# A hybrid mLSTM and attention layer on one core: the order of attention pairs, of output gates and of numerator matmuls is changed

## The chip, the core and the metric

The kernel runs on one NeuronCore of a Trainium2 chip, as one program. The time is the device time of one execution in microseconds (us), the median over runs. The engines are PE (TensorE, matmuls), ACT (ScalarE), DVE (VectorE) and the DMA queues that SP issues. Each works through its own list of instructions in order and waits on semaphores for the others.

## The reference

One trunk layer for 128 prompt tokens and 512 latent tokens, 640 in all, with the same weights:

- a half-step SwiGLU feed-forward, then two token mixers side by side, then a second half-step feed-forward;
- mixer A is a bidirectional mLSTM: for each chunk and direction the output is `num / max(|den|, exp(-m))`, where `num = (q k^T * decay) v + w * (q C)`: a part that comes from the values of the chunk, and a part that comes from the state `C` carried in;
- mixer B is grouped attention, 16 query heads on 4 key heads of 64 dimensions, rotary positions on latent tokens. Prompt tokens read the 128 prompt keys, latent tokens read 512 latent and 128 cached keys;
- `y = g0 * (hm @ w_bm) + g1 * (ha @ w_ba)`, with `hm` the mLSTM output times the sigmoid of its output gate, and then `y @ w_out`.

All weights and inputs are float32.

## The kernel before

The 640 tokens lie along the free axis, the 1024 channels in 8 blocks of 128 partitions. A projection by one block of 128 output channels is a *weight tile*: SP loads it (`raw`), ACT copies a rounded high part (`whi`, line L839), DVE subtracts for a low part (`wlo`, L1167), and PE multiplies in three terms (L458, L459, L460), twice 320 columns for each of 8 blocks. Each engine's program is a fixed list written out in order in Python; no scheduler moves anything. The attention order comes from one counter k, which every engine turns into tokens and heads for itself.

The three places that the change touches:

**The mLSTM units.** 20 units, n = 0 to 19, one for each tile of 128 tokens (5) and pair of heads (4). The first four belong to the prompt tile, which starts from no state. In each unit PE does half a weight tile, spreads m (L645, L654), multiplies keys by queries (L658), does the second half of the weight tile, and then runs `nums_of(n)`: for two heads (`hh`) and two directions (`d`) a value matmul (L670, all 128 rows of the array) and, unless c = 0, a state matmul into the same place of PSUM (L673, 64 rows: rows 0 to 63 for hh = 0, 64 to 127 for hh = 1). Every one is float32 and shows as two instructions in the trace. `turn_hm(n-1)` (L681) follows. DVE prepares `sa` and `qw` (`decays`, L1482 to L1492), and divides (`outputs`, L1501 to L1515; `scale_hm`, L1520).

**The query projections.** Ten weight tiles for keys and queries; after each one PE sums squares (L706) and swaps halves (L707), ACT forms an inverse root (`inv_rms`, L1049, L1051), and DVE rotates (`turn_halves`, L1540 to L1546).

**The attention pairs.** 40 pairs (`PAIRS`), k = 0 to 39: tile c = k // 8 (0 is the prompt), head pair m = k % 8. For each, PE computes scores (`scores`: L746 for the prompt, L751 and L754 for latent tokens, K = 64 in two halves of the array), turns the normalised weights (`turn_p`, L768: one block of 128 for each head of a prompt pair, five for a latent one) and multiplies by the values (`values`, L778). DVE takes the maximum (`top`, L1566), copies turned blocks (`take_second`, L1580, L1583), divides (`divide`, L1571, L1573) and splits the output (`low_ha`, L1590). ACT copies the other turned block (`take_p`, L1081), takes exponentials (L1094), and copies the high part (`high_ha`, L1086). On PE the order is scores(k+1), turn_p(k), [fill], values(k). A `fill` is a quarter of a weight tile of the m branch (12 matmuls, L798 to L800); there are 32, and they go beside pairs 8 to 39. The fills read h_hi and h_lo, which are made from `hm` beside the first pairs: DVE gates it (`out_gate`, L1596, pairs 0 to 7), ACT copies the high part (L1099), DVE subtracts (`low_m`, L1602, pairs 1 to 8). ACT splits a weight tile after each fourth pair (`k % 4 == 3`), DVE one pair later; `take_fill` (L1612) empties the fill's bank.

Of the kernel before, what the change touches and what calls it, by code (L numbers as in the profile page):

```python
# [17 lines left out]
ALU = mybir.AluOpType  # L18
# [3 lines left out]
P = 128  # L22
D = 1024
KC = D // P
TP, TS = 128, 512
N = TP + TS
# [36 lines left out]
UNITS = NT * 4  # L63
PAIRS = NT * KC

# [23 lines left out]
def build(nc, a):  # L89
    ctx = ExitStack()  # L90
    with ctx:
# [351 lines left out]
        def _(pe):  # L443
# [217 lines left out]
            def nums_of(n):  # L661
                c, j = n // 4, n % 4
                pe.wait_ge(s_in, n + 1)
                if n >= 1:
                    pe.wait_ge(den_s, 4 * n)
                for hh in range(2):
                    half = slice(hh * DK, (hh + 1) * DK)
                    for d in range(2):
                        out = psum[:, hh, d * (DV + 1):(d + 1) * (DV + 1)]
                        last = mm(out, sa[n % 2][:, (2 * d + hh) * P:(2 * d + hh + 1) * P], vt[:, c, 2 * j + hh, :],  # L670
                                  start=True, stop=(c == 0))
                        if c > 0:
                            last = mm(out, qw[half, n % 2, d, :], cs[half, d, c - 1, j, :], start=False, stop=True)  # L673
                last.then_inc(nums, 1)
# [34 lines left out]
            for l in range(L_AV, L_BM):  # L709
# [18 lines left out]
                if l > L_AK:  # L728
                    qk_stats(l - 1 - L_AK)
            qk_stats(QK - 1)  # L730


            def scores(k):
                c, m = k // KC, k % KC
                if k >= 1:
                    pe.wait_ge(aexp, 2 * k)
                else:
                    pe.wait_ge(ck_ev, 2)
                    pe.wait_ge(ak_sw, 32)
                    pe.wait_ge(rope_out, QK)  # L740
                half = [slice(s * HD, (s + 1) * HD) for s in range(2)]
# [19 lines left out]
            def turn_p(k):  # L761
                c = k // KC
                if k >= 1:
                    pe.wait_ge(ha_lo, k)
                for s in range(2):
                    pe.wait_ge(p_nrm, 2 * k + s + 1)
                    for b in range(1 if c == 0 else NT):
                        last = tp(turned(s, b), sa[s][:, b * P:(b + 1) * P], ident)  # L768
                    last.then_inc(atr, 1)

            def values(k):
                c, m = k // KC, k % KC
                pe.wait_ge(pta, k + 1)
# [9 lines left out]
            def fill(f):  # L783
# [17 lines left out]
                if part == 1:  # L801
                    last.then_inc(tile_done if h else half_done, 1)

            scores(0)
            for k in range(PAIRS):
                if k + 1 < PAIRS:
                    scores(k + 1)
                turn_p(k)
                if k >= KC:
                    fill(k - KC)  # L810
                values(k)
# [21 lines left out]
        def _(act):  # L833
# [219 lines left out]
            for l in range(L_AV, L_BM):  # L1053
# [17 lines left out]
                if l > L_AK:  # L1071
                    inv_rms(l - 1 - L_AK)
            inv_rms(QK - 1)

            def take_p(k):
                c = k // KC
                w = P if c == 0 else TS
# [5 lines left out]
            def high_ha(k):  # L1083
                c, m = k // KC, k % KC
                act.wait_ge(pv, k + 1)
                fn(m_hi[:, m, c * P:(c + 1) * P], psum[:, T_LAST, 2 * P:3 * P], ACT.Copy, scale=0.5).then_inc(ha_hi, 1)  # L1086

            def exponentials(k, s):
                c = k // KC
                w = P if c == 0 else N  # L1090
# [13 lines left out]

            act.preload_act_table_set("exp_and_others")
            exponentials(0, 0)
            exponentials(0, 1)
            for k in range(PAIRS):
                take_p(k)
# [46 lines left out]
        def _(dve):  # L1156
# [377 lines left out]
            scale_hm(UNITS - 1)  # L1534

            def turn_halves(e):
                dst = qk(e)
# [10 lines left out]
            for l in range(L_AV, L_BM):  # L1548
# [9 lines left out]
                if l > L_AK:  # L1558
                    turn_halves(l - 1 - L_AK)
            turn_halves(QK - 1)  # L1560


            def top(k, s):
                w = P if k < KC else N
                dve.wait_ge(sc, k + 1)
                dve.tensor_reduce(amax[:, s:s + 1], flat(s)[:, 0:w], AX.X, ALU.max, negate=True).then_inc(nmx, 1)  # L1566

            def divide(k, s):
                w = P if k < KC else N
                dve.wait_ge(aexp, 2 * k + s + 1)  # L1570
# [4 lines left out]
            def take_second(k):  # L1575
                w = P if k < KC else TS
                dve.wait_ge(atr, 2 * k + 2)
                if k >= 1:
                    dve.wait_ge(pv, k)
                last = copy(sb[1][:, 0:w], psum[:, T_BANK + 1, 0:w])  # L1580
                if k >= KC:
                    for s in range(2):
# [3 lines left out]
            def low_ha(k):  # L1586
                c, m = k // KC, k % KC
                dve.wait_ge(ha_hi, k + 1)
                cols = slice(c * P, (c + 1) * P)
                stt(m_lo[:, m, cols], psum[:, T_LAST, 2 * P:3 * P], 0.5, m_hi[:, m, cols].bitcast(F32),  # L1590
                    ALU.mult, ALU.subtract).then_inc(ha_lo, 1)

            def out_gate(m):
                dve.wait_ge(gate_in[m], 16)
                dve.wait_ge(hm_ev, UNITS)
                stt(hm[:, m, :], hm[:, m, :], 0.5, gate[m][:, :], ALU.mult, ALU.mult).then_inc(mg, 1)  # L1596
                dve.wait_ge(mg, m + 1)
                dve.sem_inc(gate_used, 1)

# [18 lines left out]
            for k in range(PAIRS):  # L1618
                top(k, 0)
                top(k, 1)  # L1620
                if k >= 1:
                    take_second(k - 1)
                divide(k, 0)
                divide(k, 1)
                if k >= 1:
                    low_ha(k - 1)
                if k < KC:
                    out_gate(k)
                if 1 <= k <= KC:
# [139 lines left out]
```

## Time and profile before

| | |
|---|---|
| time, median of 3 runs | 1977.47 us (1976.69 to 1982.18) |
| time of the profiled execution | 1979.02 us |
| its span | 1977.2 us |
| granted TensorE clock, mean | 0.972 |
| PE busy | 1873.5 us, 95% |
| DVE busy | 941.7 us, 48% |
| ACT busy | 651.2 us, 33% |
| chain that ended last | PE 86%, DVE 7%, ACT 4%, issue 2% |

PE carries the chain. Its clock has two levels; PEclk 1.00 is 2.4 GHz and 0.50 is 1.2 GHz. The mLSTM units lie from about 770 to 1011 us, the key and query projections to 1117 us, the attention pairs from 1124 to 1340 us.

### The profile page before, as it was taken

Reading aid. Unit: us, or ns where it says so; the run is one execution under the profiler, and the core shown is the slowest. Engines: PE = TensorE matmul, PEld = TensorE weight load, DVE = VectorE, ACT = ScalarE, POOL = GpSimd, SP = SyncE. Lnnn points to the kernel's source line nnn. Section 1 sums busy time; section 2 is a strip of 40 time slices with the busy share of each in tenths; the row PEclk is TensorE's granted clock in tenths of the full one; section 3 lists DMA queues with packets and bytes.
Section 4 is the critical chain, followed back from the end, with each engine's and each line's share of the span. In section 5 each row is a group of like instructions: output and inputs, shape, how many; then the busy total and the mean of one; then the engine's idle time right before and its main releaser. Section 6 shows DMA issues by size and latency. Waiting matters only on the chain.

```text
span 1977.2 us, 31472 instructions
## 1 busy us (share of the span) xinstructions
PE 1873.5 (95%) x12888; PEld 1778.8 (90%) x12888; DVE 941.7 (48%) x1578; ACT 651.2 (33%) x1067; POOL 0.2 (0%) x4
## 2 busy tenths in 40 slices
PE   6999999999968999999999789999979999999996
PEld 6999999999958998888889668889969999999996
DVE  4765465542674234444434587784354222222235
ACT  3422222112453123433323455452453222221233
POOL 0000000000000000000000000000000000000000
PEclk9999999999979999999989889999989999999997
DMA  7444444422321224222232211112312222222211
GB/s 299 148 153 129 135 157 133 133 75 95 128 85 58 72 72 98 71 69 70 70 118 83 62 52 36 36 36 71 129 43 65 74 75 75 74 75 75 72 56 54
DMA packets 52294, 178.38 MB, mean 90 GB/s; under 512 B 8521, under 2 KB 11099, under 8 KB 51427
## 3 DMA queue, kind: packets, MB, share of 16 engines
q1 hardware_dynamic: 52195, 176.97, 28.0%
q8 instruction: 72, 1.18, 0.3%
q14 instruction: 27, 0.22, 0.0%
HBM read 162.40 MB, written 13.90 MB: 89 GB/s over the span
## 4 chain that ended last, share of the span: by engine, by line
PE 86%; DVE 7%; ACT 4%; issue 2%; DMA 0%; SPq 0%; DVEq 0%; ACTq 0%
PE psum L458 22%; PE psum L460 22%; PE psum L459 22%; PE psum L778 2%; PE psum L768 2%; PE psum L500 2%; PE psum L673 1%; PE psum L751 1%; PE psum L670 1%; PE psum L489 1%; ACT whi L839 1%; DVE x L1202 1%; PE psum L645 1%; DVE macc L1231 1%; DVE amax L1566 1%
## 5 line engine op out<-in xcount | busy, mean ns | idle before, releaser
L458 PE MATMUL psum<-h_hi,whi 128*128 128x320 f32 x2288 | 718.3, 314 | 9.0 <-DVE wlo L1167 7.5
L459 PE MATMUL psum<-h_lo,whi 128*128 128x320 f32 x2288 | 708.4, 310 | 0.0
L460 PE MATMUL psum<-h_hi,wlo 128*128 128x320 f32 x2288 | 708.4, 310 | 0.0
L1167 DVE TENSOR_TENSOR wlo<-raw,whi 128x1024 fp32r<-128x1024 f32 x213 | 260.7, 1225 | 804.3 <-ACT whi L839 804.2
L458 PEld LDWEIGHTS psum<-h_hi,whi 128*128 128x128 f32 x2288 | 431.2, 188 | 15.6 <-DVE wlo L1167 7.8
L459 PEld LDWEIGHTS psum<-h_lo,whi 128*128 128x128 f32 x2288 | 431.3, 188 | 1.9 <-issue 1.9
L460 PEld LDWEIGHTS psum<-h_hi,wlo 128*128 128x128 f32 x2288 | 430.9, 188 | 0.0
L839 ACT CAST whi<-raw 128x1024 fp32r<-128x1024 f32 x213 | 222.3, 1044 | 380.4 <-PE psum L460 370.2
L458 PE MATMUL psum<-g_hi,whi 128*128 128x320 f32 x704 | 218.2, 310 | 1.2 <-DVE g_lo L1296 1.2
L459 PE MATMUL psum<-g_lo,whi 128*128 128x320 f32 x704 | 217.6, 309 | 0.0
L460 PE MATMUL psum<-g_hi,wlo 128*128 128x320 f32 x704 | 217.5, 309 | 0.0
L1231 DVE SCALAR_TENSOR_TENSOR macc<-mw,silc,macc 128x512 f32<-128x512 f32 x210 | 142.7, 744 | 0.0
L458 PEld LDWEIGHTS psum<-g_hi,whi 128*128 128x128 f32 x704 | 132.3, 188 | 1.7 <-DVE g_lo L1296 1.7
L459 PEld LDWEIGHTS psum<-g_lo,whi 128*128 128x128 f32 x704 | 132.2, 188 | 0.0
L460 PEld LDWEIGHTS psum<-g_hi,wlo 128*128 128x128 f32 x704 | 132.2, 188 | 0.0
L917 ACT ACTIVATE sa<-psum 128x640 f32<-128x640 f32 x44 | 31.0, 705 | 151.4 <-PE psum L460 148.4
L778 PE MATMUL psum<-sb,av 128*64 128x128 f32 x672 | 47.3, 284 | 18.3 <-DVE sb L1580 12.4
L923 ACT CAST g_hi<-sb 128x640 f32 x44 | 32.1, 729 | 93.2 <-DVE sb L1290 93.2
L778 PEld LDWEIGHTS psum<-sb,av 128*64 128x64 f32 x672 | 37.0, 139 | 27.6 <-issue 26.5
L1094 ACT ACTIVATE sa<-psum,amax 128x640 f32<-128x640 f32 (+1 forms) x80 | 56.1, 709 | 13.1 <-DVE amax L1566 13.1
L1566 DVE TENSOR_REDUCE amax<-psum 128x1 f32<-128x640 f32 (+1 forms) x80 | 53.5, 711 | 14.0 <-PE psum L754 12.7
L1296 DVE TENSOR_TENSOR g_lo<-sb,g_hi 128x640 f32 x44 | 36.2, 823 | 36.8 <-ACT g_hi L923 36.8
(218 smaller groups left out, 2027.0 us busy)
## 6 DMA issues: line engine op xcount, KB each, us to landing
raw<-in_w_ffn_in SPq DMA_DIRECT2D x88, 512.0 KB, 3.5
raw<-in_w_mix SPq DMA_DIRECT2D x77, 512.0 KB, 3.7
mw<-in_w_mod SPq DMA_DIRECT2D x28, 768.0 KB, 4.7
raw<-in_w_ffn_out SPq DMA_DIRECT2D x32, 512.0 KB, 3.5
mw<-in_w_mod SPq DMA_DIRECT2D x4, 2048.0 KB, 19.5
gate<-gate_keep SPq DMA_DIRECT2D x24, 320.0 KB, 4.1
mw<-in_w_mod SPq DMA_DIRECT2D x14, 512.0 KB, 3.7
gate_keep<-gate SPq DMA_DIRECT2D x20, 320.0 KB, 4.6
```

Of the source, the lines that this page charges most:

```text
L458: mm(out, whi[t.slot][:, k, :], hi[:, k, cols], start=(k == 0), stop=False)
L459: mm(out, whi[t.slot][:, k, :], lo[:, k, cols], start=False, stop=False)
L460: last = mm(out, wlo[t.slot][:, k, :], hi[:, k, cols], start=False, stop=(k == nk - 1))
L500: last = mm(mod_out(2 * t + g, bank), macc[:, g, t * P:(t + 1) * P], ones_d, start=True, stop=True)
L768: last = tp(turned(s, b), sa[s][:, b * P:(b + 1) * P], ident)
L778: last = mm(psum[s * HD:(s + 1) * HD, T_LAST, 2 * P:3 * P], av[:, v, (m // 2) * HD:(m // 2 + 1) * HD], sb[s][:, b * P:(b + 1) * P], start= ...
L839: copy(whi[t.slot][:, :, :], raw[t.raw][:, :, :]).then_inc(w_hi, 1)
L1094: fn(sa[s][:, 0:w], flat(s)[:, 0:w], ACT.Exp, bias=amax[:, s:s + 1], accum_out=asum[:, s:s + 1]).then_inc(aexp, 1)
L1167: tt(wlo[t.slot][:, :, :], raw[t.raw][:, :, :], whi[t.slot][:, :, :].bitcast(F32), ALU.subtract).then_inc(raw_free, 1)
L1231: last = stt(acc, w[:, k, :], by, acc, ALU.mult, ALU.add)
L1296: tt(g_lo[:, jj, :].rearrange("p o n -> p (o n)"), sb[s][:, :], g_hi[:, jj, :].rearrange("p o n -> p (o n)").bitcast(F32), ALU.subtract).t ...
L1566: dve.tensor_reduce(amax[:, s:s + 1], flat(s)[:, 0:w], AX.X, ALU.max, negate=True).then_inc(nmx, 1)
```

## The change

Three edits, in all engines' lists alike:

1. A table `ORDER` gives tile and heads for each pair. Pairs 0 to 7 are now those of the first latent tile. After them come 8 groups of four: three latent pairs and one prompt pair. The fills stay at pairs 8 to 39, ACT's weight splits at `k % 4 == 3`, which is now the prompt pair of each group. The scores of the first pair stand ahead of the last square sum and rotation.
2. `out_gate(m)` is done beside the eight query projections and no longer beside pairs 0 to 7.
3. In `nums_of`, both heads' value matmuls come first, then both heads' state matmuls of direction 0, those of direction 1, and then the value matmuls of direction 1.

```diff
+ORDER = [(1, m) for m in range(KC)]
+for i in range(KC):
+    ORDER += [(2 + n // KC, n % KC) for n in range(3 * i, 3 * i + 3)] + [(0, i)]
+PAIRS = len(ORDER)
...
@@ PE, nums_of
-                for hh in range(2):
-                    half = slice(hh * DK, (hh + 1) * DK)
-                    for d in range(2):
-                        out = psum[:, hh, d * (DV + 1):(d + 1) * (DV + 1)]
-                        last = mm(out, sa[...], vt[:, c, 2 * j + hh, :], start=True, stop=(c == 0))
-                        if c > 0:
-                            last = mm(out, qw[half, n % 2, d, :], cs[half, d, c - 1, j, :], start=False, stop=True)
+                for d in range(2):
+                    for part in ((0, 1) if d == 0 else (1, 0)):
+                        for hh in range(2):
...
@@ PE, scores
-                    pe.wait_ge(rope_out, QK)
+                if k < KC:
+                    pe.wait_ge(rope_out, NKC + m + 1)
@@ PE, turn_p
+                else:
+                    pe.wait_ge(rope_out, QK)
@@ PE
-            qk_stats(QK - 1)
+            for l in (L_BM - 2, L_BM - 1):
+                t = Tile(T_MIX + l)
+                pe.wait_ge(ev[t.slot], t.pair + 1)
             scores(0)
+            qk_stats(QK - 1)
@@ ACT
-            inv_rms(QK - 1)
-            act.preload_act_table_set("exp_and_others")
             exponentials(0, 0)
             exponentials(0, 1)
+            inv_rms(QK - 1)
+            act.preload_act_table_set("exp_and_others")
@@ DVE, beside the projections
-            turn_halves(QK - 1)
+                if l >= L_AQ:
+                    out_gate(l - L_AQ)
@@ DVE, the pairs
                 if k >= 1:
                     take_second(k - 1)
+                else:
+                    turn_halves(QK - 1)
...
-                if k < KC:
-                    out_gate(k)
```

What stands on PE in one mLSTM unit, before (n = 4; L670 are value matmuls, L673 state matmuls, L681 the turn of the unit before):

```order
L670 MATMUL psum<-vt,sa_70 128x129
L673 MATMUL psum<-cs,qw 128x129
L670 MATMUL psum<-vt,sa_70 128x129
L673 MATMUL psum<-cs,qw 128x129
L670 MATMUL psum<-vt,sa_70 128x129
L673 MATMUL psum<-cs,qw 128x129
L670 MATMUL psum<-vt,sa_70 128x129
L673 MATMUL psum<-cs,qw 128x129
L681 MATMUL psum<-cst,hmt 128x128 x2
L458 MATMUL psum<-h_hi,whi_67 128x320
```

and after, at the same place (the lines are now L675, L678, L686, L461):

```order
L463 MATMUL psum<-h_hi,wlo_68 128x320
L675 MATMUL psum<-vt,sa_70 128x129 x2
L678 MATMUL psum<-cs,qw 128x129 x4
L675 MATMUL psum<-vt,sa_70 128x129 x2
L686 MATMUL psum<-cst,hmt 128x128 x2
L461 MATMUL psum<-h_hi,whi_67 128x320
```

The eight matmuls are the same; between 128 rows and 64 rows the list changed eight times (the change to L681 counted), and now it changes twice.

What stands on DVE where the projections end and the pairs begin, before (L1540 to L1546 rotate the last queries, L1566 is the maximum of pair 0, L1596 the gate):

```order
L1540 TENSOR_TENSOR sb_72<-psum,cst 128x512
L1541 TENSOR_TENSOR aq<-aq,cst 128x512
L1543 TENSOR_TENSOR aq<-aq,sb_72 128x512
L1546 TENSOR_TENSOR aq<-aq,rb 128x640
L1566 TENSOR_REDUCE amax<-psum 128x1 x2
L1571 RECIPROCAL arec<-asum 128x1
L1573 TENSOR_SCALAR sa_70<-sa_70,arec 128x128
L1571 RECIPROCAL arec<-asum 128x1
L1573 TENSOR_SCALAR sa_71<-sa_71,arec 128x128
L1596 SCALAR_TENSOR_TENSOR hm<-hm,gate_119 128x640
L1566 TENSOR_REDUCE amax<-psum 128x1 x2
```

and after (L1550 is the last gate, L1585 the maximum, L1558 to L1564 the last rotation, L1590 and L1592 the division of pair 0):

```order
L1550 SCALAR_TENSOR_TENSOR hm<-hm,gate_126 128x640
L1585 TENSOR_REDUCE amax<-psum 128x1 x2
L1558 TENSOR_TENSOR sb_72<-psum,cst 128x512
L1559 TENSOR_TENSOR aq<-aq,cst 128x512
L1561 TENSOR_TENSOR aq<-aq,sb_72 128x512
L1564 TENSOR_TENSOR aq<-aq,rb 128x640
L1590 RECIPROCAL arec<-asum 128x1
L1592 TENSOR_SCALAR sa_70<-sa_70,arec 128x640
L1590 RECIPROCAL arec<-asum 128x1
L1592 TENSOR_SCALAR sa_71<-sa_71,arec 128x640
L1585 TENSOR_REDUCE amax<-psum 128x1 x2
```

The eighth gate and the first maximum now stand ahead of the last rotation, and the first pair is a latent one (640 columns instead of 128).

## Rows read from the trace of the kernel before

**Rows 1.** Busy time by stage: stretch, length, PE, PEld, DVE, ACT, POOL, PEclk, DMA share, GB/s.

```profile
885.00:1005.00 120.00, 118.83 (x713) 101.97 (x712) 52.53 (x142) 37.43 (x101) 0.00 (x0) 1.00 0.23 66
1127.00:1152.00 25.00, 13.98 (x72) 7.35 (x68) 21.49 (x68) 12.84 (x47) 0.00 (x0) 0.50 0.33 92
1158.00:1330.00 172.00, 166.14 (x1624) 148.59 (x1622) 136.80 (x324) 84.95 (x195) 0.00 (x0) 1.00 0.11 36
```

**Rows 2.** Timeline, PE, unit 9, numerators: start, duration, instruction, [idle before].

```profile
886.20 0.38 PE L670 MATMUL psum<-vt,sa 128*128 128x129 f32 x2
886.51 0.49 PE L673 MATMUL psum<-cs,qw 64*128 64x129 f32 x2
...
889.43 0.44 PE L681 MATMUL psum<-cst,hmt 128*128 128x128 f32 x2
```

**Rows 3.** Timeline, PE, a unit of the prompt tile, value matmuls alone.

```profile
801.49 1.05 PE L670 MATMUL psum<-vt,sa 128*128 128x129 f32 x8
802.38 0.38 PE L681 MATMUL psum<-cst,hmt 128*128 128x128 f32 x2
```

**Rows 4.** Timeline, PE, two K = 64 matmuls side by side, then the projection.

```profile
882.16 0.49 PE L658 MATMUL psum<-mq,mk 64*128 64x128 f32 x4
882.58 0.41 PE L458 MATMUL psum<-h_hi,whi 128*128 128x320 f32 x1
```

**Rows 5.** Timeline, DVE and PE around the numerators of that unit.

```profile
883.66 0.75 DVE L1492 TENSOR_TENSOR sa<-sa,psum 128x256 f32<-128x256 f32 x2 [0.37 <-ACT sa L1007]
888.06 1.23 DVE L1167 TENSOR_TENSOR wlo<-raw,whi 128x1024 fp32r<-128x1024 f32 x1 [3.65 <-ACT whi L839]
892.68 0.42 DVE L1520 TENSOR_TENSOR hmt<-hmt,ss 128x256 f32<-128x256 f32 x1 [1.33 <-ACT ss L1018]
893.31 1.12 PE L645 MATMUL psum<-nm,rowc 8*128 8x256 f32 x4
```

**Rows 6.** Timeline of the last unit on PE, and the clock of the stretch it starts in.

```profile
1004.82 0.77 PE L670 MATMUL psum<-vt,sa 128*128 128x129 f32 x2 [1.17 <-DVE sb L1510]
...
1010.61 0.69 PE L681 MATMUL psum<-cst,hmt 128*128 128x128 f32 x2
```

```profile
1004.00:1008.00 4.00, 3.18 (x9) 2.30 (x10) 1.52 (x4) 1.71 (x8) 0.00 (x0) 0.58 0.75 213
```

**Rows 7.** Timeline, PE and DVE, the first scores and the second pair's maximum.

```profile
1124.43 0.80 PE L746 MATMUL psum<-ak,aq 64*128 64x128 f32 x4 [3.06 <-DVE aq L1546]
...
1127.85 0.49 DVE L1566 TENSOR_REDUCE amax<-psum 128x1 f32<-128x128 f32 x2 [0.15 <-DVE hm L1596]
```

**Rows 8.** Timeline, a latent pair with a fill (k = 10 and its neighbours), PE and DVE.

```profile
1161.38 1.31 PE L778 MATMUL psum<-sb,av 128*64 128x128 f32 x20
1162.62 1.14 PE L751 MATMUL psum<-ak,aq 64*128 64x256 f32 x8
1163.90 1.31 PE L768 MATMUL psum<-cst,sa 128*128 128x128 f32 x10
1164.02 1.55 DVE L1566 TENSOR_REDUCE amax<-psum 128x1 f32<-128x640 f32 x2 [0.69 <-PE psum L754]
1166.09 0.48 DVE L1583 COPY sb<-psum 128x128 f32<-128x128 f32 x2
1166.91 1.31 PE L778 MATMUL psum<-sb,av 128*64 128x128 f32 x20
```

**Rows 9.** Timeline, DVE, maximum of the last pair, k = 39.

```profile
1330.63 1.55 DVE L1566 TENSOR_REDUCE amax<-psum 128x1 f32<-128x640 f32 x2 [0.29 <-PE psum L754]
```

**Rows 10.** Timeline, ACT and DVE, the cast and subtraction of hm beside a prompt pair.

```profile
1148.48 0.72 ACT L1099 CAST h_hi<-hm 128x640 fp32r<-128x640 f32 x1
...
1149.78 0.83 DVE L1602 TENSOR_TENSOR h_lo<-hm,h_hi 128x640 fp32r<-128x640 f32 x1
```

**Rows 11.** The scores of the first latent pair, and the clock behind them.

```profile
1151.97 2.08 PE L751 MATMUL psum<-ak,aq 64*128 64x256 f32 x8
```

```profile
1154.00:1156.00 2.00, 1.02 (x8) 0.48 (x4) 1.86 (x3) 0.88 (x2) 0.00 (x0) 0.80 0.63 161
```

More of the change, by code:

```diff
@@ L63 @@
 UNITS = NT * 4
-PAIRS = NT * KC
+ORDER = [(1, m) for m in range(KC)]
+for i in range(KC):
+    ORDER += [(2 + n // KC, n % KC) for n in range(3 * i, 3 * i + 3)] + [(0, i)]
+PAIRS = len(ORDER)
 STATES = ((0, 0), (1, 0), (0, 1), (1, 4), (0, 2), (1, 3), (0, 3), (1, 2))
@@ L665, in nums_of @@
                     pe.wait_ge(den_s, 4 * n)
-                for hh in range(2):
-                    half = slice(hh * DK, (hh + 1) * DK)
-                    for d in range(2):
-                        out = psum[:, hh, d * (DV + 1):(d + 1) * (DV + 1)]
-                        last = mm(out, sa[n % 2][:, (2 * d + hh) * P:(2 * d + hh + 1) * P], vt[:, c, 2 * j + hh, :],
-                                  start=True, stop=(c == 0))
-                        if c > 0:
-                            last = mm(out, qw[half, n % 2, d, :], cs[half, d, c - 1, j, :], start=False, stop=True)
+                for d in range(2):
+                    for part in ((0, 1) if d == 0 else (1, 0)):
+                        for hh in range(2):
+                            half = slice(hh * DK, (hh + 1) * DK)
+                            out = psum[:, hh, d * (DV + 1):(d + 1) * (DV + 1)]
+                            if part == 0:
+                                last = mm(out, sa[n % 2][:, (2 * d + hh) * P:(2 * d + hh + 1) * P], vt[:, c, 2 * j + hh, :],
+                                          start=(d == 0 or c == 0), stop=(d == 1 or c == 0))
+                            elif c > 0:
+                                mm(out, qw[half, n % 2, d, :], cs[half, d, c - 1, j, :], start=(d == 1), stop=(d == 0))
                 last.then_inc(nums, 1)
@@ L729, in _ @@
                     qk_stats(l - 1 - L_AK)
-            qk_stats(QK - 1)
             def scores(k):
-                c, m = k // KC, k % KC
+                c, m = ORDER[k]
                 if k >= 1:
@@ L761, in turn_p @@
             def turn_p(k):
-                c = k // KC
+                c = ORDER[k][0]
                 if k >= 1:
                     pe.wait_ge(ha_lo, k)
+                else:
+                    pe.wait_ge(rope_out, QK)
                 for s in range(2):
@@ L771, in values @@
             def values(k):
-                c, m = k // KC, k % KC
+                c, m = ORDER[k]
                 pe.wait_ge(pta, k + 1)
@@ L1072, in _ @@
                     inv_rms(l - 1 - L_AK)
-            inv_rms(QK - 1)
             def take_p(k):
-                c = k // KC
+                c = ORDER[k][0]
                 w = P if c == 0 else TS
@@ L1083, in high_ha @@
             def high_ha(k):
-                c, m = k // KC, k % KC
+                c, m = ORDER[k]
                 act.wait_ge(pv, k + 1)
@@ L1088, in exponentials @@
             def exponentials(k, s):
-                c = k // KC
+                c = ORDER[k][0]
                 w = P if c == 0 else N
@@ L1534, in _, with out_gate @@
             scale_hm(UNITS - 1)
+            def out_gate(m):
+                dve.wait_ge(gate_in[m], 16)
+                dve.wait_ge(hm_ev, UNITS)
+                stt(hm[:, m, :], hm[:, m, :], 0.5, gate[m][:, :], ALU.mult, ALU.mult).then_inc(mg, 1)
+                dve.wait_ge(mg, m + 1)
+                dve.sem_inc(gate_used, 1)
             def turn_halves(e):
@@ L1559, in _ @@
                     turn_halves(l - 1 - L_AK)
-            turn_halves(QK - 1)
+                if l >= L_AQ:
+                    out_gate(l - L_AQ)
             def top(k, s):
-                w = P if k < KC else N
+                w = P if ORDER[k][0] == 0 else N
                 dve.wait_ge(sc, k + 1)
@@ L1568, in divide @@
             def divide(k, s):
-                w = P if k < KC else N
+                w = P if ORDER[k][0] == 0 else N
                 dve.wait_ge(aexp, 2 * k + s + 1)
@@ L1575, in take_second @@
             def take_second(k):
-                w = P if k < KC else TS
+                w = P if ORDER[k][0] == 0 else TS
                 dve.wait_ge(atr, 2 * k + 2)
@@ L1580, in take_second @@
                 last = copy(sb[1][:, 0:w], psum[:, T_BANK + 1, 0:w])
-                if k >= KC:
+                if ORDER[k][0]:
                     for s in range(2):
@@ L1586, in low_ha @@
             def low_ha(k):
-                c, m = k // KC, k % KC
+                c, m = ORDER[k]
                 dve.wait_ge(ha_hi, k + 1)
@@ L1591, in low_ha @@
                     ALU.mult, ALU.subtract).then_inc(ha_lo, 1)
[L1593 to L1598, printed above, removed]
             def low_m(m):
```

## The prediction

> **What bounds the kernel.** I read the busy time by stage first, then the timeline of each stage that the change touches. In the mLSTM stage PE is busy 118.83 of 120 us at a clock of 1.00, and DVE and ACT have room: what PE saves there the kernel saves, as long as nothing else becomes late [rows 1]. In the attention stage with fills PE is busy 166.14 of 172 us. Beside the prompt pairs it is busy 13.98 of 25 us and the clock stands at 0.50: there DVE (21.49 us) sets the pace, and PE has idle time that fills cannot use, since they wait for `hm` to be split [rows 1]. So the numerators are a matter of PE time, and the new order a matter of where idle PE time lies and which clock it brings.
>
> **Numerators.** From the first value matmul at 886.20 to the turn at 889.43 the eight matmuls (16 instructions) of a unit take 3.23 us, 0.20 each [rows 2]. In a unit of the prompt tile eight such instructions in a row take 802.38 - 801.49 = 0.89 us, 0.11 each [rows 3]. The shape is the same, so half of the 3.23 us goes with the changes between 128 and 64 rows: 3.23 - 16 x 0.11 = 1.5 us over 8 changes, 0.19 each. The two K = 64 matmuls of the key-query product (4 instructions, one per half of the array, as the new state matmuls alternate) take 882.58 - 882.16 = 0.42 us with the change behind them, so 0.22 for four instructions: they run side by side, else it would be 0.44 + 0.19 [rows 4]. After the change a unit has four value matmuls, 8 x 0.11 = 0.88; four state matmuls in two pairs, 0.43; two changes, 0.38: 1.7 us. It saves 1.55, with rounding and the slower turn behind the last change (which goes too) 1.6 us.
>
> The Trainium skill (TensorEngine Tiling (Array Packing), Key Properties) says that changing the tiling mode, not just the tile, drains the engine; this agrees with 0.19 us for each change here. The same page (Gotcha 1: PSUM Pressure) says that different row tiles cannot write one PSUM bank at a time; here the two heads write banks 0 and 1, so by that rule too the pairs overlap.
>
> 16 units have state matmuls. Does DVE keep up? Its weight split stands ahead of `outputs` in its list and ends at 888.06 + 1.23 = 889.29, tied to the half tile before the numerators, not to them [rows 5]. Before, `outputs` began just after, with the end of the numerators. Now these end at 887.9, but `outputs` still begins at 889.3, 0.25 earlier than before. Its chain ends with `scale_hm` at 893.10 before and 892.85 now; the next `decays` needs that, and the spread m, which PE had ready some 1.2 us after 893.31 and now has 1.6 earlier, at 892.9. The two meet, and behind them is slack: `decays` ended at 884.41 for numerators that began at 886.20, 1.8 us later [rows 2, 5]. So 15 units save 1.6 us each, 24 us. Unit 19 is different: nothing stands between the numerators of 18 and 19 but `outputs(18)`, and that hangs on the weight split of DVE. It starts where it did, after a longer wait. Before, it waited 1.17 us and then ran from 1004.82 to 1010.61, 5.8 us, with a clock of 0.58 in that stretch [rows 6]; at the low level the new order costs twice 1.55 us, 3.1, and saves 2.7. **Sum: -27 us.** Bounds: -18 if only the drains go (6 x 0.19 x 16) and the state matmuls do not overlap; -30 if the clock stays up in unit 19 and behind it.
>
> **The gates.** Eight times 0.82 us of DVE move from the prompt pairs to the projections (the row of the same size is the subtraction, 0.83) [rows 10]. A projection takes PE about 9 us, and DVE's split, rotation and gate are some 5 us, so there it costs nothing. Only the eighth stands in the way, ahead of the first maximum.
>
> **The start.** Before, the last rotation ended at 1124.43 and the maximum of pair 1 began at 1127.85 [rows 7]. Now the rotation comes behind a gate (0.8) and two maxima of 640 columns (1.5): it ends 2.3 later, 1126.7, with some 0.2 of ACT waiting (its exponentials stand ahead of the inverse root) at 1126.9. Then two divisions of 640 columns, 1.3 us (an estimate, 2.5 times the 128-column ones is an upper bound), and the maximum of pair 1 begins at 1128.2. That is **+0.3 us**, with one latent pair half done instead of a prompt pair.
>
> **The pairs 1 to 10.** Before, from 1127.85 to the maximum of pair 10 at 1164.02: 36.2 us [rows 7, 8]. Now pairs 1 to 8 are latent (pairs 1 to 7 have no fill). What is the period of a latent pair without a fill? A closed loop goes from the first maximum to the last copy of turned blocks, 1166.57 - 1164.02 = 2.55; 0.15 to PE; values 1162.62 - 1161.38 = 1.24, and 0.12 to ACT (as from scores to maximum: 1.40 for 1.28) [rows 8]; `high_ha`, which holds ACT 0.2; the cast of hm, 0.72; the subtraction on DVE, 0.83 [rows 10]; then the next maximum. That is 5.8, and with the ends that overlap (0.1) **5.7 us**, while PE works 1.28 (scores) + 1.05 (turns, ten instructions of 0.11) + 1.24 = 3.6 of it. So the nine periods from pair 1 to pair 10 (eight like this, the last 5.3 without cast) are 51 us: **+15 us** at full clock.
>
> **The clock.** It is low at the start in both (0.50 beside the prompt pairs [rows 1], and the scores of a latent pair then take 2.08 for 1.14 [rows 8, 11]). With all PE times doubled a loop is values 2.5, scores 2.5, turns 2.1, copies and ways 1.5: 8.6 us, 2.9 more than at full clock. Before, the clock rose between 1154 and 1156, just behind the first latent pair's scores [rows 11], so here it should rise within the first two pairs: +5. But PE then idles 2.1 us in each 5.7, in one piece ahead of the values, and in the last mLSTM unit a wait of 1.17 us behind the drained numerators was followed by the low level [rows 6]. I take it to fall again once or twice, two slow pairs in all: +5. **Sum +9 us**; bounds 0 (high all along) and 8 x 2.9 = +23 (low all along).
>
> **The groups of four, pairs 10 to 39.** Before 1330.63 - 1164.02 = 166.6 us for 29 periods, 5.75 each, of which PE's work is 1166.91 - 1161.38 = 5.53 [rows 8, 9]; the rest, 0.9 us in four pairs, comes with the weight split on ACT and DVE. Now one in four is a prompt pair, one block for five: it takes off 0.95 of scores, 4/5 of 1.05 and of 1.24 of turns and values, 2.8 us. PE's work for a group is 4 x 5.53 - 2.8 = 19.3. I laid the three lists beside one another with these durations: the values behind the split still wait 0.8, since DVE takes the split ahead of the next maximum and its copies; and 0.7 more is lost where a latent pair follows a prompt pair, because PE's share of these iterations (3.7 and 4.6 us) is shorter than DVE's round of maximum, copies, divisions (5 us). 20.9 us for a group; 7.25 groups, 151.5: **-15 us**. Bounds: 19.3 (-27) and 22.1, no shorter than four latent pairs of 5.53 (-6). The last pair is a prompt pair, whose turns and values are not hidden: 0.84 + 1.0 shorter, **-2 us**.
>
> The attention stage in all: +0.3 + 15 + 9 - 15 - 2 = +7 us. With -27 it is -20: 1979.0 - 20 = 1959 in the profiled execution, whose time stands 1.5 us above the median of the runs (1977.5); so **1957.5 us**. What a measurement can tell from no change is 0.3%, 6 us.
>
> **The rivals.**
> - *The clock stays high in the new latent pairs* (0.22). For it: in the whole fill stage it is at 1.00 with PE idle 3% [rows 1]. Against: 2.1 us idle in each pair. Then +9 becomes +1 to +3: 1950.
> - *It stays low for most of the eight* (0.15). For it: with 14 of 25 us busy it stayed at 0.50 throughout [rows 1]. Against: at the low level these pairs keep PE 7.1 of 8.6 us busy, and it rose behind a single latent pair's scores. +23 for +9: 1971.
> - *The units save less, or DVE becomes their bound* (0.08): two chains meet within 0.1 us at `decays`, and 1.8 us of slack is all there is. With 1.1 for 1.6 us: 1966.
> - *The prompt pairs don't shorten their groups* (0.07): the wait moves from PE's work to DVE's round, a group stays at 22.1. -6 for -15: 1967.
> - *Slower* (0.04): the cost of a 64-row instruction is its own (it shows in both instructions of each pair, not only at the change), so the order of the numerators gives under 0.3 us a unit, -5; with the clock low for all eight pairs, the stage gives +21. 1995. It decides from 0.9 us a unit down with a low clock. Rows 3 speak against, as do rows 4.
>
> **The chances.** The forecast has 0.44 and its own range 1952 to 1965. The range of 8 in 10 takes in the high clock and most of the low one: 1946 to 1972. Faster by over 0.3% (below 1971.5) is the forecast, the high clock, both small rivals, and half of the low clock: 0.89. Within 0.3%: 0.07. Slower: 0.04.
>
> **What would show it.** In the profile after: a unit with one row of four, one of eight and one of four numerator instructions, 1.6 to 1.8 us from first to turn, and 11.0 us from unit to unit for 12.64; `outputs` right behind the weight split; the last unit's start near its old distance from unit 18's end plus 1.6. Pair periods of 5.7 (clock 1.00) or 8.6 (0.50) in the first eight, and how many of each; groups of 20.9 us with a wait ahead of the values behind each split. It is wrong if units still are over 12 us apart, if the eight pairs take over 70 us or under 45, or if groups are at 22 or at 19.5.

## The result and the profile after

The changed kernel takes 1950.63 us (median of 4 runs, 1950.55 to 1955.21), the kernel before 1978.37 beside it: ratio 0.9863, 95% interval 0.9849 to 0.9878. That is 27.7 us less; forecast were 20. The time lies inside the range of 8 in 10 (1946 to 1972) and 1.4 us below the forecast's own range (1952 to 1965), where the prediction has its rival of a high clock (1950). The profiled execution took 1955.21 us, the slowest of the four, 4.6 above their median, with a span of 1953.4 for 1977.2. Cut at marks that both traces have:

| stretch | before, us | after, us | difference | forecast |
|---|---|---|---|---|
| to the first spread of unit 0 | 769.66 | 770.66 | +1.0 | 0 |
| to the last turn, behind unit 19 | 250.2 | 223.7 | -26.5 | -27 |
| to the maximum of pair 1 | 108.0 | 108.4 | +0.4 | +0.3 |
| pair 1 to pair 10 | 36.2 | 53.3 | +17.2 | +24 (15 + 9) |
| pair 10 to pair 39 | 166.6 | 152.6 | -14.0 | -15 |
| from there to the end | 646.6 | 644.7 | -1.9 | -2 |
| span | 1977.2 | 1953.4 | -23.8 | -20 |

The first line is code that did not change; how much it varies, the first `outputs` shows: it stands at 785.3 us before, 786.3 after, and 782.1 in the first experiment, with the same instructions ahead of it. Such a difference can be the 4 us between the 23.8 of the traces and the 27.7 of the medians; the other executions of the changed kernel have no trace that would show it.

The busy time by stage, against [rows 1]: stretch, length, PE, PEld, DVE, ACT, POOL, PEclk, DMA share, GB/s. They are a piece of the mLSTM units, the latent pairs without fills, and the groups.

```profile
877.00:977.00 100.00, 100.00 (x687) 90.89 (x686) 49.15 (x136) 35.83 (x99) 0.00 (x0) 1.00 0.27 78
1103.00:1156.00 53.00, 39.05 (x389) 33.05 (x388) 42.59 (x98) 27.70 (x63) 0.00 (x0) 0.92 0.01 2
1156.00:1308.00 152.00, 142.52 (x1336) 125.38 (x1334) 115.61 (x296) 74.27 (x188) 0.00 (x0) 1.00 0.12 41
```

The middle row is the surprise: clock 0.92. Four slow pairs of 8.6 us in 60, which the forecast added up to, would give 0.71 (an estimate from its own terms).

The numerators of unit 9 in the timeline of PE (start, duration, instruction), against [rows 2]:

```profile
879.43 0.61 PE L675 MATMUL psum<-vt,sa 128*128 128x129 f32 x4
879.97 0.72 PE L678 MATMUL psum<-cs,qw 64*128 64x129 f32 x8
880.61 0.71 PE L675 MATMUL psum<-vt,sa 128*128 128x129 f32 x4
881.16 0.38 PE L686 MATMUL psum<-cst,hmt 128*128 128x128 f32 x2
```

From the first to the turn 881.16 - 879.43 = 1.73 us for 3.23. Eight value instructions take 0.88 of it and two changes 0.4, which leaves 0.45 for the eight state instructions: half of 8 x 0.11.

Is it the change of shape that costs, or that a state matmul adds into the place of PSUM that the value matmul ahead of it has just written? In the same unit before, each block of two instructions begins 0.42 us behind the last, whichever way it goes:

```profile
886.93 0.49 PE L670 MATMUL psum<-vt,sa 128*128 128x129 f32 x2
887.34 0.49 PE L673 MATMUL psum<-cs,qw 64*128 64x129 f32 x2
887.76 0.49 PE L670 MATMUL psum<-vt,sa 128*128 128x129 f32 x2
```

From L670 to L673 the place is the same, from L673 to the next L670 it is another, and both take 2 x 0.11 and 0.20. The change of shape carries the price, then, and not the shared place.

What DVE does around it, with PE's spread of m between, against [rows 5]:

```profile
881.30 1.23 DVE L1178 TENSOR_TENSOR wlo<-raw,whi 128x1024 fp32r<-128x1024 f32 x1 [3.65 <-ACT whi L850]
882.44 0.15 DVE L1512 SCALAR_TENSOR_TENSOR den<-psum,tk 128x4 f32<-128x4 f32 x1
...
884.99 1.12 PE L648 MATMUL psum<-nm,rowc 8*128 8x256 f32 x4
...
885.57 0.42 DVE L1531 TENSOR_TENSOR hmt<-hmt,ss 128x256 f32<-128x256 f32 x1 [1.33 <-ACT ss L1029]
...
886.15 1.13 DVE L1493 SCALAR_TENSOR_TENSOR sa<-psum,tk,cst 128x128 f32<-128x128 f32 x4 [0.16 <-PE psum L648]
```

`outputs` (L1512) now begins right behind the weight split, 1.3 us after its numerators ended. DVE is done with `scale_hm` (L1531) at 885.99 and waits 0.16 us for the spread: the two chains meet within 0.2 us, as forecast, and the distance from unit to unit is 11.09 us (12.64 before).

The last unit, against [rows 6], and its clock:

```profile
983.73 0.68 PE L675 MATMUL psum<-vt,sa 128*128 128x129 f32 x4 [2.39 <-DVE sb L1521]
...
986.24 0.64 PE L686 MATMUL psum<-cst,hmt 128*128 128x128 f32 x2
```

```profile
984.00:988.00 4.00, 4.00 (x23) 3.65 (x22) 1.84 (x8) 1.71 (x8) 0.00 (x0) 0.58 0.59 184
```

It waits 2.39 us for 1.17, falls to the low level in the middle, and takes 2.5 us for 5.8. Behind it the clock is at 0.98 again from 988 to 990 us; before, it stood at 0.50 from 1006 to 1014. That brings the last turn another 1.1 us nearer (8.12 us behind this one for 9.24).

The latent pairs without fills: the maxima of pairs 1, 2 and 3 on DVE, and PE's scores and values between them.

```profile
1102.77 1.54 DVE L1585 TENSOR_REDUCE amax<-psum 128x1 f32<-128x640 f32 x2
...
1105.97 2.40 PE L785 MATMUL psum<-sb,av 128*64 128x128 f32 x20 [1.27 <-DVE sb L1602]
...
1108.30 2.08 PE L756 MATMUL psum<-ak,aq 64*128 64x256 f32 x8
...
1110.86 1.56 DVE L1585 TENSOR_REDUCE amax<-psum 128x1 f32<-128x640 f32 x2 [0.70 <-PE psum L759]
...
1113.55 1.31 PE L785 MATMUL psum<-sb,av 128*64 128x128 f32 x20 [1.41 <-DVE sb L1602]
1114.79 1.13 PE L756 MATMUL psum<-ak,aq 64*128 64x256 f32 x8
...
1119.25 1.31 PE L785 MATMUL psum<-sb,av 128*64 128x128 f32 x20 [1.86 <-DVE sb L1602]
```

```profile
1116.57 0.82 DVE L1585 TENSOR_REDUCE amax<-psum 128x1 f32<-128x640 f32 x1
```

The first period, 8.09 us, runs at the low level (scores 2.08, values 2.40); the second, at the high one, takes 5.71, and so do all that follow up to pair 9 (5.70). From the third period on PE waits 1.86 us in one piece ahead of the values; the forecast had 2.1. The clock rose in this stretch:

```profile
1110.00:1112.00 2.00, 2.00 (x16) 1.59 (x14) 1.30 (x3) 0.37 (x1) 0.00 (x0) 0.76 0.00 0
```

The periods of a group are 5.15, 5.39, 5.19 and 5.33 us, 21.06 in all; the last maximum, against [rows 9], is one of 128 columns:

```profile
1308.69 0.48 DVE L1585 TENSOR_REDUCE amax<-psum 128x1 f32<-128x128 f32 x2
```

### The profile page after: what moved, and what is told of

Its sections match the earlier page's. It is cut to its first block, busy times and chain, and to the rows that moved or that the text cites. A ratio compares the mean times of both kernels' runs of the same rounds, so it can differ in the third digit from the quotient of the medians.

```text
span 1953.4 us, 31481 instructions
## 1 busy us (share of the span) xinstructions
PE 1844.7 (94%) x12888; PEld 1764.6 (90%) x12888; DVE 940.2 (48%) x1578; ACT 651.6 (33%) x1067; POOL 0.2 (0%) x4
## 4 chain that ended last, share of the span: by engine, by line
PE 83%; DVE 9%; ACT 4%; issue 3%; DMA 0%; SPq 0%; DVEq 0%; ACTq 0%
PE psum L461 23%; PE psum L462 22%; PE psum L463 22%; PE psum L785 2%; PE psum L503 2%; DVE amax L1585 1%; PE psum L775 1%; PE psum L492 1%; PE psum L756 1%; PE psum L675 1%; DVE x L1213 1%; PE psum L648 1%; DVE macc L1242 1%; DVE wlo L1178 1%; ACT whi L850 1%
## 5 line engine op out<-in xcount | busy, mean ns | idle before, releaser
L461 PE MATMUL psum<-h_hi,whi 128*128 128x320 f32 x2288 | 719.0, 314 | 9.0 <-DVE wlo L1178 7.5
L461 PEld LDWEIGHTS psum<-h_hi,whi 128*128 128x128 f32 x2288 | 431.7, 189 | 15.6 <-DVE wlo L1178 7.8
L461 PE MATMUL psum<-g_hi,whi 128*128 128x320 f32 x704 | 218.3, 310 | 1.2 <-DVE g_lo L1307 1.2
L461 PEld LDWEIGHTS psum<-g_hi,whi 128*128 128x128 f32 x704 | 132.3, 188 | 1.7 <-DVE g_lo L1307 1.7
L1585 DVE TENSOR_REDUCE amax<-psum 128x1 f32<-128x640 f32 (+1 forms) x80 | 53.5, 710 | 11.2 <-PE psum L759 11.1
L1307 DVE TENSOR_TENSOR g_lo<-sb,g_hi 128x640 f32 x44 | 36.2, 823 | 36.8 <-ACT g_hi L934 36.8
```

Of the source, the lines that this page charges most:

```text
L461: mm(out, whi[t.slot][:, k, :], hi[:, k, cols], start=(k == 0), stop=False)
L1307: tt(g_lo[:, jj, :].rearrange("p o n -> p (o n)"), sb[s][:, :], g_hi[:, jj, :].rearrange("p o n -> p (o n)").bitcast(F32), ALU.subtract).t ...
```

## The experiments

All times are medians; the ratio is to the kernel before on the same chip, with its 95% interval. The kernel before itself took 1978.4 us beside the changed kernel, 1979.1 beside e1 to e4, 1981.9 beside e5 to e8 and 1980.3 beside e9 and e10, so kernels of different groups are compared by the ratio. The last column leaves out the stretch ahead of the mLSTM units, which no edit touches and which took 766 to 771 us: it is the time in the trace from the first spread of unit 0 to the end.

| kernel | us | ratio (interval) | from unit 0 to the end, trace |
|---|---|---|---|
| kernel before | 1978.4 | 1 | 1207.6 |
| changed kernel | 1950.6 | 0.9863 (0.9849 to 0.9878) | 1182.8 |
| e1, numerators alone | 1951.1 | 0.9867 (0.9850 to 0.9883) | 1182.9 |
| e2, pairs and gates alone | 1980.8 | 1.0009 (0.9999 to 1.0018) | 1212.1 |
| e3, prompt pairs first | 1950.0 | 0.9853 (0.9837 to 0.9870) | 1178.8 |
| e4, heads apart | 1966.9 | 0.9945 (0.9928 to 0.9962) | 1195.7 |
| e5, gates back | 1955.6 | 0.9878 (0.9862 to 0.9893) | 1187.4 |
| e6, e3 and the split one pair later | 1943.0 | 0.9810 (0.9797 to 0.9824) | 1171.4 |
| e7, states by head | 1952.1 | 0.9858 (0.9840 to 0.9875) | 1182.8 |
| e8, outputs first | 1950.0 | 0.9843 (0.9826 to 0.9860) | 1180.5 |
| e9, e6 and e8 | 1939.8 | 0.9796 (0.9780 to 0.9811) | 1168.9 |
| e10, changed kernel, both moves on DVE | 1946.0 | 0.9828 (0.9813 to 0.9843) | 1177.1 |

**e1: the numerators alone.** The kernel before with `nums_of` of the changed one.

> The kernel before with the new order of the numerators alone. My theory: the order of the numerators carries nearly the whole gain. The trace after shows units 11.09 us apart for 12.64, 1.55 each, and the last unit 2.7 shorter; that is 26 us, so this kernel stands 24 to 27 us below the kernel before, near 1952. Rival: part of the gain comes from the moved gates and the new pairs; then this kernel gains under 20 us and the pairs alone over 5.

It gains 28 us, all that the changed kernel gains (24.7 us in the trace from unit 0 on, 24.8 there). Its units are 11.09 us apart; its pairs run as before (3.78 us beside the prompt, 36.2 us from pair 1 to pair 10). The rival is out.

**e2: pairs and gates alone.** The changed kernel with the old `nums_of`.

> The changed kernel with the old order of the numerators: new order of the pairs, gates beside the projections. My theory, from the two traces: start +0.3, pairs 1 to 10 +17.2, groups -14.0, end -1.9, in all +1.6 us over the kernel before, within what can be measured, -2 to +4. Rival, by the forecast's +7 for this stage (the clock falls again in the latent pairs in most executions, and the profiled one was lucky): +5 to +9. Second rival: the pairs alone gain over 5.

1.7 us slower than before, at the edge of what ten runs tell from nothing. The stage is a wash, as the table of stretches has it (+1.7). The profiled execution is the slowest of the ten, and its trace is 4.5 us above the one before from unit 0 on: 1.5 of it are a stretch at the low level inside the first units (0.60 from 776 to 780 us), and 1.4 the latent pairs. But the clock is not steady: of the nine periods from pair 1 to 10 this profile has 8.09, 6.08, 6.31 and 6.13 beside 5.70. The fall behind the wait of pair 5, in the timeline of PE and the windows:

```profile
1157.63 1.31 PE L783 MATMUL psum<-sb,av 128*64 128x128 f32 x20 [1.86 <-DVE sb L1600]
1158.87 1.91 PE L754 MATMUL psum<-ak,aq 64*128 64x256 f32 x8
```

```profile
1158.00:1160.00 2.00, 2.00 (x24) 1.67 (x22) 1.16 (x5) 0.89 (x2) 0.00 (x0) 0.77 0.00 0
1160.00:1162.00 2.00, 2.00 (x12) 1.62 (x11) 1.48 (x3) 0.00 (x0) 0.00 (x0) 0.50 0.00 0
1162.00:1164.00 2.00, 1.09 (x8) 0.85 (x6) 1.68 (x5) 1.50 (x4) 0.00 (x0) 0.88 0.00 0
```

The wait of 1.86 us ahead of it is no longer than those of the pairs before (1.87 and 1.86 at 1146.22 and 1151.92), behind which the clock stayed at 1.00, and the same as in the changed kernel. So the length of the wait does not tell when the clock falls; what does, no run here shows. The level was back about 3 us later, and a fall cost 0.4 to 0.6 us, since it covers part of a pair, and a part that had idle time. The forecast priced each at 2.9.

**e3: the prompt pairs first.**

```diff
-ORDER = [(1, m) for m in range(KC)]
-for i in range(KC):
-    ORDER += [(2 + n // KC, n % KC) for n in range(3 * i, 3 * i + 3)] + [(0, i)]
+ORDER = [(c, m) for c in range(NT) for m in range(KC)]
```

> The changed kernel with ORDER in the old sequence (prompt pairs first); the moved gates and the new numerators stay. My theory: the gates' 0.82 us on DVE were on the path beside the prompt pairs, where DVE was busy 21.5 of 25 us, so their period falls from 3.78 to about 3.0 even at the low clock; pairs 1 to 10 take 31 us for 53, pairs 10 to 39 again 166.6 for 152.6. That is 5 to 8 us less than the changed kernel, near 1944. Rival: a prompt pair's period is not DVE's work but a loop through PE at the low clock, and stays near 3.7; then this kernel is level with the changed one (-2 to +1).

Level with the changed kernel. Neither theory fits: the period of a prompt pair did fall, from 3.78 to 3.22 us (3.0 forecast), 3.1 us over the six of them from pair 1 on. But the clock, low beside the prompt pairs, rose later than before: the two periods ahead of pair 10 took 5.13 and 6.24 us for 4.15 and 5.34, which gives 1.9 back. These are windows of e3 and of e6, which runs the same instructions up to there:

```profile
1126.00:1130.00 4.00, 3.71 (x19) 2.80 (x20) 3.08 (x8) 1.80 (x6) 0.00 (x0) 0.50 0.00 0
```

```profile
1122.00:1126.00 4.00, 2.67 (x16) 1.61 (x14) 3.06 (x6) 1.85 (x5) 0.00 (x0) 0.71 0.00 0
```

In e6 the same pairs took 4.15 and 5.35, so when the clock rises differs from execution to execution by some 4 us. From pair 1 to pair 10 the two took 35.0 and 33.0 us, against 53.3 in the changed kernel; from pair 10 to 39 e3 took 166.6 against 152.6, and the end is 1.9 longer. Ahead of pair 1 it is 1.6 us shorter, since the first pair is a prompt pair. The sum, 3.9 us less by the traces (1178.8 for 1182.8), is what the intervals leave open: the medians differ by 0.6, the ratios by 2.0.

**e4: the heads apart.** The loops of `nums_of` turned: `for hh` outside, `for d` and `for part` inside, so value, state, state, value for head 0 and then for head 1.

> The changed kernel with the numerators of head 0 first (value, state, state, value) and then those of head 1: four changes between 128 and 64 rows for two, and no two state matmuls on different halves of the array next to each other. My theory (0.19 us for a change, and two state matmuls side by side cost as one): a unit's eight matmuls take 16 x 0.11 + 4 x 0.19 = 2.5 us for 1.7, units 11.9 us apart, +0.8 x 15 and 1.6 for the last = +13 us over the changed kernel. Rival A, all of it the changes, no overlap: +0.38 a unit, +6 us. Rival B, the count of changes costs nothing and only the overlap gains: a unit is as long as before, +27.

Units are 11.92 us apart for 11.09: +0.83, and the whole is +16 us by the medians, +12.9 by the traces, where the units give 10.9 and a low clock in the latent pairs 2.0. The theory's 0.8 holds, rivals A (0.38) and B (1.55) don't. In the trace each block of two matmuls (four instructions) takes the same, whatever its rows:

```profile
880.11 0.71 PE L675 MATMUL psum<-vt,sa 128*128 128x129 f32 x4
880.75 0.71 PE L678 MATMUL psum<-cs,qw 64*128 64x129 f32 x4
881.39 0.49 PE L675 MATMUL psum<-vt,sa 128*128 128x129 f32 x2
```

0.64 us from block to block of four instructions, 4 x 0.11 and one change of 0.2: two states of one head do not overlap. So of the 1.55 us a unit, 6 changes give 1.1 to 1.2 and the overlap of two halves 0.4.

**e5: the gates back beside pairs 0 to 7.**

> The changed kernel with the eight gates back on DVE beside pairs 0 to 7 (now latent pairs). My theory: beside the projections the gates cost nothing; beside latent pairs DVE is in a closed loop (copies, values on PE, high part and cast on ACT, subtraction) in which it waits 0.42 us for the cast, so of the gate's 0.74 us only 0.3 to 0.4 lengthen a period: 6.05 for 5.70, about +3 us over the changed kernel, less 0.8 at the start. Rival A: all of it is on the path, +6. Rival B: the gates are hidden beside latent pairs too, 0.

+3 us over the changed kernel by the ratios, +4.6 by the traces: periods of 6.25 us for 5.70, 0.55 each for the 0.3 to 0.4 expected. Six of them give 3.3 us; a low clock in two pairs (7.57 and 6.76 us) adds 1.8, and the first slow period is 0.5 shorter. The first maximum stands 0.9 us earlier, but the period behind it is as much longer. Rival A is not excluded by the time alone, but by the periods. In DVE's timeline of one pair the gate (L1550) takes its 0.8 and 0.15 more until the subtraction may read `hm`, and only the 0.42 of waiting for the cast is gained back:

```profile
1122.85 0.29 DVE L1607 SCALAR_TENSOR_TENSOR m_lo<-psum,m_hi 128x128 fp32r<-128x128 f32 x1 [0.49 <-ACT m_hi L1096]
1123.06 0.81 DVE L1550 SCALAR_TENSOR_TENSOR hm<-hm,gate 128x640 f32<-128x640 f32 x1
1124.02 0.83 DVE L1612 TENSOR_TENSOR h_lo<-hm,h_hi 128x640 fp32r<-128x640 f32 x1
1124.76 1.55 DVE L1583 TENSOR_REDUCE amax<-psum 128x1 f32<-128x640 f32 x2
```

The move of the gates is worth 3 to 5 us, then. This kernel differs from e1 by the new order of the pairs alone (and the first scores and rotation that go with it), and is 4.5 us above it in the trace, with a ratio of 0.9878 for 0.9867: without the move the new order is a loss.

**e6: DVE's weight split one pair later, on e3.**

```diff
-                    if f % 4 == 3:
-                        split(Tile(T_MIX + L_BM + f // 4 + 2))
+                if k > KC + 1 and k % 4 == 1:
+                    split(Tile(T_MIX + L_BM + (k - KC - 2) // 4 + 2))
```

> e3_prompt_first with DVE's weight splits beside the fills one pair later (k % 4 == 1 for 0), in the iteration without take_fill. My theory: the long period of each group (6.62 us) comes from DVE, which has split (1.14), take_fill (0.42) and a latent pair's 4.0 us in one iteration; with the split in the next one each fits into 5.53, a group takes 22.1 for 23.0 us, -6 us against e3, near 1944. Rival: the long period comes from the wait for ACT's cast of the weights ahead of it, then moving DVE's part changes nothing (-1 to +1).

1943.0, 7 us under e3 (8.5 by the ratios, 7.4 by the traces), of which 5.2 are the groups: periods of 5.52, 5.89, 5.33, 5.52 us, 22.3 for 23.0, and 1.9 the earlier rise of the clock. DVE around a split in e3, where `take_fill` (L1622), the wait for the cast and the split stand ahead of the maximum:

```profile
1151.57 0.48 DVE L1622 SCALAR_TENSOR_TENSOR y<-gate,psum 128x320 f32<-128x320 f32 x1
1152.29 1.23 DVE L1176 TENSOR_TENSOR wlo<-raw,whi 128x1024 fp32r<-128x1024 f32 x1 [0.25 <-ACT whi L848]
1153.43 1.55 DVE L1583 TENSOR_REDUCE amax<-psum 128x1 f32<-128x640 f32 x2
```

and in e6, where the split stands ahead of the maximum without `take_fill` and without a wait:

```profile
1154.55 1.22 DVE L1176 TENSOR_TENSOR wlo<-raw,whi 128x1024 fp32r<-128x1024 f32 x1
1155.68 1.55 DVE L1583 TENSOR_REDUCE amax<-psum 128x1 f32<-128x640 f32 x2
```

**e7: the states by head.** Two value matmuls, the states of head 0 in both directions, those of head 1, two value matmuls.

> The changed kernel with the four state matmuls in the order head 0, head 0, head 1, head 1: two changes of shape as now, but only one neighbour pair on different halves of the array. My theory: side by side they cost as one only where neighbours alternate, so a unit's states take three slots of 0.22 for two; units 11.3 us apart for 11.09, +3.5 us. Rival: neither matters once they stand together (PE reorders for itself), 0. Second rival: no overlap at all here, +0.43 a unit, +7.

Units stay 11.09 us apart, and the trace from unit 0 on is as long as that of the changed kernel to 0.1 us. My theory fell. The eight instructions take 0.65 us as in the changed kernel, though four on one half of the array stand ahead of four on the other:

```profile
888.46 0.60 PE L670 MATMUL psum<-vt,sa 128*128 128x129 f32 x4
889.00 0.72 PE L679 MATMUL psum<-cs,qw 64*128 64x129 f32 x8
889.65 0.71 PE L670 MATMUL psum<-vt,sa 128*128 128x129 f32 x4
```

With e4 (0.64 for four on one half alone) this says that work on both halves overlaps inside one block of the same shape, not only between neighbours. In the records the eight begin two by two, 0.01 us apart, where the four of e4 begin 0.11 apart or more. How the engine does it, no run here shows.

**e8: DVE's outputs ahead of the weight split.**

```diff
             for n in range(UNITS):
                 if n >= 1:
                     outputs(n - 1)
+                    split(Tile(T_MIX + L_MO + RING + 2 + n))
                     scale_hm(n - 1)
                 if n + 1 < UNITS:
                     decays(n + 1)
-                    split(Tile(T_MIX + L_MO + RING + 3 + n))
```

> The changed kernel with DVE's outputs of a unit ahead of the weight split, which moves between outputs and scale_hm of the same unit. My theory: the period of a unit stays 11.09 (PE's work), and only the last unit gains, which waits for outputs(18): it starts 1.2 us earlier, and with a shorter wait the clock may stay up: -1 to -4 us. Rival: units in the middle gain too, since outputs and decays meet within 0.1 us; then they are under 11.0 apart and it is more than -5.

The trace has what the theory says, and more. Units with state matmuls stay 11.09 apart. The last unit starts 4.5 us behind the one before in the changed kernel and 3.4 here, the clock stays at 1.00 through it, and from its first value matmul to the turn it takes 2.27 us for 2.51:

```profile
979.98 0.68 PE L675 MATMUL psum<-vt,sa 128*128 128x129 f32 x4 [1.32 <-DVE sb L1521]
```

With the work behind it at the full clock too, that is 2.2 us. The other 1.9 us neither the theory nor the rival has: two periods in the prompt tile are shorter, 9.83 us for 10.81 and 10.26 for 11.23. There `outputs` came long after its numerators in the changed kernel: unit 0 starts them at 781.85 us, `outputs` stood behind the weight split until 786.29, and a unit later PE waited 0.75 us at 793.72. Here `outputs` begins 1.1 us behind the first value matmul, and that wait is gone. All units together, from the first spread to the last turn, take 4.1 us less (219.6 for 223.7). By the ratios the kernel is 4 us faster than the changed kernel (0.9843 for 0.9863, and the intervals meet). Its trace shows 2.2, since the profiled execution also has three periods lengthened by a low clock (6.17, 6.22 and 6.26 us for 5.70, 5.70 and 5.33).

**e9 and e10: the parts together.** e9 is e6 with e8's edit; e10 is the changed kernel with both edits.

> Three parts that gained, together: e6_split_moved (prompt pairs first, gates beside the projections, DVE's weight split one pair later, new numerators) and DVE's outputs ahead of the weight split as in e8_outputs_first. My theory: they lie in different stages and add up; the last unit starts 0.8 us earlier than in e6, so -1 to -2 against it, near 1942. Rival: the clock turns the gain over again (a start of the stage at another moment), then it is anywhere from -3 to +3 around 1943.

> The changed kernel (latent pairs first, one prompt pair in each group) with DVE's weight split one pair later and DVE's outputs ahead of the weight split in the mLSTM units. My theory: in the groups of four the wait of 0.8 us behind the split goes, but the rest of the 21.06 us is DVE's and PE's rounds one after the other, so a group takes 20.3 us, -5 us against the changed kernel, and -1 for the last unit: near 1945, not better than the prompt pairs first. Rival: the split beside a latent pair instead of behind the prompt pair finds less room and the group stays at 21: 1949 to 1951.

e9 takes 1939.8 us, the fastest of all, 3 below e6 (2.8 by the ratios, 2.5 by the traces, all of it in the units), a little more than the 1 to 2 expected. e10 is 6.9 under the changed kernel by the ratios, 5.7 by the traces. Its groups have periods of 5.39, 4.04, 5.82, 4.96, 20.2 us, as expected: a prompt pair now shortens its iteration to 4.0. But eight latent pairs without fills cost it more than that gains: 56.3 us from pair 1 to pair 10 for 33.1 in e9, and 146.6 for 161.5 from 10 to 39.

## Why the prediction was right, and where it was off

**The numerators: right in mechanism and size.** 1.73 us for the eight matmuls (1.7 forecast), 1.55 a unit saved (1.6), -26.5 us for -27. In the last unit the sum is right by offsets: the forecast let the unit's wait grow but charged nothing for it (it grew by 1.2), and it took the low-level cost as twice 1.55, the saving, where twice the new 1.7 would be 3.4. Against that the unit became 3.3 us shorter for 2.7, since only part of it ran at the low level, and the work behind it 1.1 us shorter. That the price sat in the changes of shape and in the overlap of the halves was read from two rows of 128 and 64 rows alone [rows 3, 4]; e1 shows the whole, e4 both parts apart, and the blocks of 0.42 us before rule out the shared place in PSUM. Only the condition for the overlap was too narrow (e7).

**Does DVE keep up: right.** The chains meet within 0.2 us in the units with state matmuls. That DVE's weight split cost 2 us in the prompt tile, before and after, the prediction did not see; e8 shows it.

**The gates and the start: right.** +0.4 for +0.3; e5 shows that the gates were not free elsewhere.

**Pairs 1 to 10 at the high clock: right.** 5.70 us a period for 5.7, from a closed loop laid out of rows, with PE waiting 1.86 us in it (2.1).

**The clock: the step that was off.** "I take it to fall again once or twice, two slow pairs in all: +5", after another +5 for two slow pairs at the start. There was one slow pair at the start, +2.4, and none behind it in this profile; the term measured 2.2 us for 9, 6.8 less. Without these 6.8 the forecast would have been 1951. That this meets the 1950.6 measured is in part chance: the traces differ by 23.8 us, and such a forecast by 26.8. The rival "the clock stays high in the new latent pairs" was the true case in this profile, at 0.22. The falls do come (e2, e4, e5, e8, e10), but in the profiles of these kernels, they cost 0.2 to 1.3 us a period, and 1.4 to 2.9 us from pair 1 to pair 10 (54.8 in e2, 56.3 in e10, for 53.3): the engine waits 1.86 of 5.70 us, so part of a slower matmul fills idle time, and the level came back within a few us. The price of a whole pair at the low clock was the wrong price for a fall. The sign that the forecast went by, the wait, was no sign either: 1.17 us before the last unit was followed by the low level, 1.32 in e8 was not, and 1.86 in the latent pairs was at 1157.63 us in e2, but in the changed kernel never was.

**The groups: right.** 21.06 us for 20.9. e6 and e10 show the wait behind the split as a cost of its own (0.74 to 0.85 us a group). The rival of a group that stays at 22.1 is out.

Of the three edits the numerators give the gain; the new order of pairs and the gates cancel. With the prompt pairs first, the moved gates and the earlier first scores are worth 1 to 4 us (e3 against e1: 1.1 by the medians, 2.8 by the ratios, 4.1 by the traces).

## What to carry to other kernels

Before an engine's list is called full, divide its busy time by its instructions and look for the same shape elsewhere in the trace: 0.20 us here and 0.11 there was the whole of this gain. Compare small differences in traces, from a mark behind the code that did not change: here that code alone varied by 4 us. Put matmuls of one array shape together, and small ones that use different halves inside the same block. Idle time that is filled in one stage may be made in another: add up the periods on both sides of a reordering, and when pricing a clock that may fall, price the time until it is back and not the whole stretch, less the idle time that it fills.

## What the hardware showed unexpectedly

- Eight float32 instructions of 64 rows took 0.45 us when four and four were on different halves of the array, in whichever order inside the block (changed kernel, e7), and four on one half 0.44 (e4); both are what is left of 0.64 to 0.65 us from block to block, with 0.2 for a change.
- The granted clock of one and the same list of instructions rose at about 1124 us in one execution (e6) and after 1130 in another (e3).
- The same wait of 1.86 us ahead of the values was followed by the low level at 1157.63 us in e2, but not at 1151.92 in the same execution, nor at any of six such waits in the changed kernel.
- Executions of the same instructions ahead of the first mLSTM unit took 766.2 to 770.7 us in twelve traces.
